# Stick-breaking attention's causal mask: moved from TensorE's products to a GpSimd multiplication

## The reference

```python
for blk in range(T // Q_BLOCK):            # Q_BLOCK = 128 queries
    s0 = blk * Q_BLOCK
    end = s0 + Q_BLOCK
    logits = jnp.einsum("bhtd,bhsd->bhts", q[:, :, s0:end], kb) * (Dh ** -0.5)
    mask = s_idx[None, :] < t_idx[:, None]
    log_keep = jnp.where(mask, jax.nn.log_sigmoid(-logits), 0.0)
    after = jnp.sum(log_keep, axis=-1, keepdims=True) - jnp.cumsum(log_keep, axis=-1)
    wts = jnp.where(mask, jnp.exp(jax.nn.log_sigmoid(logits) + after), 0.0)
    outs.append(jnp.einsum("bhts,bhsd->bhtd", wts, vb))
```

## Time and profile before

| | |
|---|---|
| Median of 3 runs | 1159.59 us (1159.42 to 1159.63) |
| The profiled execution | 1159.38 us, of which the trace's span is 1157.6 us |
| Busy share of the span | PE 96%, PEld 76%, DVE 45%, ACT 44%, POOL 32% |
| Mean granted TensorE clock | 0.991 of full speed |
| First and last of the 64 products with `bandbf` | start at 622.2 and 692.0 us |
| Loads of 1 MB into `raw` for `w_out_b` | 5.2 us from issue to landing |
| ScalarE's split of `D_OUTB + 1`, slot 1 | starts at 721.5 us |

### The profile page before, as it was taken

The page is one execution under the profiler, slowest core; times in us unless marked ns, Lnnn a source line. Parts: engine busy times, 40 slices in busy tenths (PEclk is TensorE's granted clock), DMA queues, the critical chain, the costliest instruction groups (busy, mean ns, idle before and its releaser), DMA issues.

```text
span 1157.6 us, 20420 instructions
## 1 busy us (share of the span) xinstructions
PE 1114.9 (96%) x8466; PEld 879.9 (76%) x8466; DVE 516.1 (45%) x938; ACT 514.7 (44%) x907; POOL 371.1 (32%) x148
## 2 busy tenths in 40 slices
PE   5999999989999999999999999999999999999998
PEld 3688886767768889777776668888877777678767
DVE  4575553455543366242234882853013332331562
ACT  5223226753335534453365883433335434753530
POOL 0134342232246341434334001333343213433260
PEclk7999999999999999999999999999999999999999
DMA  9822331276751132234522101322232322224201
GB/s 315 261 69 83 109 100 46 73 256 210 231 185 38 38 109 64 83 98 139 128 73 73 38 1 37 109 86 79 91 102 59 107 80 72 75 79 156 97 1 73
DMA packets 103004, 119.32 MB, mean 103 GB/s; under 512 B 4679, under 2 KB 89207, under 8 KB 102791
## 3 DMA queue, kind: packets, MB, share of 16 engines
q1 hardware_dynamic: 99054, 115.08, 31.4%
q10 hardware_dynamic: 3864, 3.01, 0.9%
HBM read 110.75 MB, written 2.10 MB: 97 GB/s over the span
## 4 chain that ended last, share of the span: by engine, by line
PE 83%; ACT 6%; DVE 5%; issue 3%; DMA 1%; ACTq 1%; SPq 0%; POOL 0%; DVEq 0%
PE ps L2079 43%; PE ps L2876 4%; PE ps L2125 2%; PE ps L2472 2%; PE ps L2686 2%; PE ps L2721 2%; PE ps L2498 2%; PE ps L2163 1%; PE ps L2704 1%; PE ps L2220 1%; PE ps L2243 1%; PE ps L2296 1%; PE ps L2842 1%; PE ps L2829 1%; DMA ada_a<-in_w_ada_dram 1%
## 5 line engine op out<-in xcount | busy, mean ns | idle before, releaser
L615 POOL TENSOR_TENSOR wlo<-raw,whi 128x2048 fp32r<-128x2048 f32 x53 | 245.3, 4629 | 525.6 <-ACT whi L781 513.1
L781 ACT ACTIVATE whi<-raw 128x2048 fp32r<-128x2048 f32 x52 | 99.3, 1912 | 191.7 <-PE ps L2079 152.6
L621 POOL TENSOR_TENSOR wlo<-raw,whi 128x2048 fp32r<-128x2048 f32 x10 | 46.4, 4639 | 112.0 <-ACT whi L870 63.5
L1809 DVE TENSOR_TENSOR_SCAN taken<-kept,taken 128x255 f32<-128x255 f32 (+2 forms) x64 | 51.2, 852 | 21.4 <-ACT taken L1200 21.4
L1290 ACT ACTIVATE p<-sc,nmx 128x256 f32<-128x256 f32 x64 | 32.0, 501 | 45.9 <-PE ps L2829 44.7
L1906 DVE CUSTOM_DVE_ANT_0 sc<-ps,biast 128x256 f32<-128x256 f32 (+1 forms) x64 | 22.4, 393 | 65.7 <-PE ps L2818 36.8
L870 ACT ACTIVATE whi<-raw 128x2048 fp32r<-128x2048 f32 x11 | 21.1, 1917 | 63.2 <-PE ps L2079 63.2
L2079 PE MATMUL ps<-hC_hi,whi 128*128 128x512 f32 x184 | 47.0, 397 | 0.8 <-POOL wlo L615 0.8
L2079 PE MATMUL ps<-hC_lo,whi 128*128 128x512 f32 x184 | 45.5, 390 | 0.0
L2079 PE MATMUL ps<-hC_hi,wlo 128*128 128x512 f32 x184 | 45.4, 389 | 0.0
L2079 PEld LDWEIGHTS ps<-hC_hi,whi 128*128 128x128 f32 x184 | 33.7, 188 | 14.8 <-issue 6.4
(11 more groups left out here) (504 smaller groups left out, 2641.9 us busy)
## 6 DMA issues: line engine op xcount, KB each, us to landing
raw<-in_w_in_dram SPq DMA_DIRECT2D x24, 1024.0 KB, 5.1
raw<-in_w_in_a_dram SPq DMA_DIRECT2D x16, 1024.0 KB, 5.6
raw<-in_w_ada_dram SPq DMA_DIRECT2D x8, 1024.0 KB, 5.1
late_w<-in_w_ada_dram SPq DMA_DIRECT2D x8, 1024.0 KB, 5.7
raw<-in_w_kv_dram SPq DMA_DIRECT2D x8, 1024.0 KB, 5.2
raw<-in_w_in_b_dram SPq DMA_DIRECT2D x8, 1024.0 KB, 6.0
ada_a<-in_w_ada_dram SPq DMA_DIRECT2D x4, 1024.0 KB, 10.2
ada_b<-in_w_ada_dram SPq DMA_DIRECT2D x4, 1024.0 KB, 12.9
```

What stands on the lines that cost most here:

```text
L615: pool.tensor_tensor(wlo[:, s, :], raw[:, s, :], whi[:, s, :].bitcast(F32), ALU.subtract).then_inc(lo_ready, 1)
L621: pool.tensor_tensor(wlo[:, s, :], raw[:, s, :], whi[:, s, :].bitcast(F32), ALU.subtract).then_inc(lo_ready, 1)
L781: A(whi[:, s, :], raw[:, s, :], ACT.Copy).then_inc(hi_ready, 1)
L1809: last = dve.tensor_tensor_scan(taken[:, r % 3, keys], kept[:, r % 3, keys], taken[:, r % 3, keys], 0.0, ALU.mult, ALU.add)
```

## The change

The mask no longer goes through the logits. TensorE's products with `bandbf` are left out, with the two casts that made that tile and the wait on them. Instead GpSimd multiplies the diagonal tiles of `taken` by a table of 0 and 1 (`earlier`, 1 where the key is before the query), in place, for both heads in one instruction, and VectorE's scans wait for `masked` where they waited for `taken_done`. `kept` isn't masked any more: over the masked keys the scan's state is still 0, whatever `kept` holds there. In GpSimd's queue the 24 rounds of masks stand between `split_lo(D_OUTB, 0)` and `split_lo(D_OUTB, 1)`.

```diff
-for _name, _n in (("ident", 128), ("band", 128), ("eps", 1), ...
+for _name, _n in (("ident", 128), ("earlier", 128), ("eps", 1), ...
...
-    put("band", np.where(p < c, 0.0, -BIG))
+    put("earlier", p > c)
...
-        bandbf = sb("bandbf", [128, 2, 128], BF16)
...
+            def mask(r):
+
+                pool.wait_ge(taken_done, r + 1)
+                for i, at in round_tiles(r):
+                    keys = of_round(taken, r)[:, :, at + 128 * i:at + 128 * i + 128]
+                    last = pool.tensor_tensor(keys, keys, C("earlier").unsqueeze(1).broadcast_to([128, 2, 128]), ALU.mult)
+                last.then_inc(masked, 1)
+
             split_lo(D_OUTB, 0)
+            for r in range(ROUNDS):
+                mask(r)
             split_lo(D_OUTB, 1)
...
             dve.wait_ge(cst_loaded, 16)
-            copy(bandbf[:, 0, :], ident)
-            copy(bandbf[:, 1, :], C("band")).then_inc(bf_ready, 1)
...
-            dve.wait_ge(bf_ready, 3)
+            dve.wait_ge(bf_ready, 2)
...
                 dve.wait_ge(kept_done, r + 1)
-                dve.wait_ge(taken_done, r + 1)
+                dve.wait_ge(masked, r + 1)
...
             pe.wait_ge(kqn_done, 16)
-            pe.wait_ge(bf_ready, 1)
...
                     for e in range(2):
-                        mm(logits(r)[:, e, at:at + 128 * i + 128], qTb[side(e), kt, 128 * i:128 * i + 128],
+                        last = mm(logits(r)[:, e, at:at + 128 * i + 128], qTb[side(e), kt, 128 * i:128 * i + 128],
                            kTb[side(e), kt, 0:128 * i + 128], start=at == 0, stop=True, skip_group_check=True)
-                for i, at in round_tiles(r):
-                    for e in range(2):
-                        last = mm(logits(r)[:, e, at + 128 * i:at + 128 * i + 128], bandbf[:, 1, :], bandbf[:, 0, :],
-                                  start=False, stop=True, skip_group_check=True)
                 last.then_inc(scores_full, 1)
```

More of the change, by code:

```diff
@@ L31 @@
 _at = 0
-for _name, _n in (("ident", 128), ("band", 128), ("eps", 1), ("first32", 1), ("ones", 128), ("onesbd", 128), ("tri", 128), ("half0", 128), ("half1", 128),
+for _name, _n in (("ident", 128), ("earlier", 128), ("eps", 1), ("first32", 1), ("ones", 128), ("onesbd", 128), ("tri", 128), ("half0", 128), ("half1", 128),
                   ("decmask", 64), ("m1t", 64), ("id64", 64), ("lev", 32 * len(LEVELS)), ("negtri", 128), ("negones", 128), ("swap", 128),
@@ L426, in mixer_stack @@
         picks_ready, last_silu = sem("picks_ready"), sem("last_silu")
-        cz_done = sem("cz_done")
+        cz_done, masked = sem("cz_done"), sem("masked")
         v_moved = [sem(f"v_moved{s}") for s in range(2)]
```

## The result

The changed kernel took 1170.59 us (median of 4 runs, 1168.9 to 1172.9), the kernel before 1159.51 us (4 runs, 1158.83 to 1159.63): a ratio of 1.0093, 95% interval 1.0078 to 1.0108. It is slower by some 11 us. The forecast was 1167.2 us, in a range of 1161.0 to 1170.5; the direction held, and the median lies 3.4 us above the forecast, at the upper end of the range (0.1 us beyond it).

The account below looks back on a forecast made before the run. TensorE bounds the kernel before, at 8.62 us a pair; VectorE and GpSimd together become the bound. Start and pairs +1.5, queueing at the end +4.35, clock +1.8 give +7.65, 1167.2 us against the median; range 1161 to 1170.5.

Parts of the forecast that it names:

- Exclusion of two-input instructions: Attention loop: GpSimd masks exclude VectorE's scans and `yb_low`, but not `yb`; an inserted mask costs 0.50 us.
- the list of signs: What would show it: scans in rounds 3 to 22 taking 0.5 us or more over their old 1.2, 0.94 and 0.6.
- the layout: One head pair retimed from A's first scan (rounds A: r % 3 = 0, then B, C), masks inserted: 9.26 us.
- Rival 1: Attention loop: masks hidden, TensorE still the bound, pairs of 7.9 us, about 1155 us in all; chance 0.06.
- TensorE would need 7.85 us a pair: Attention loop: dropping 64 bf16 products takes 0.77 us per pair off TensorE's 8.62.
- The pair: Attention loop: a head pair takes 9.2 us instead of 8.62, five pairs adding 2.9 us.
- The start, -1.4: Start of the loop: the split leaves, some masks come in; round 6's scans start at 644.2 instead of 645.58 us.
- The end, 4.35 us of queueing: End of the loop: `split_lo(D_OUTB, 1)` runs right behind round 23's masks, before its scans; 4.35 of +5.85 us.
- Rival 2: End of the loop: VectorE keeps the port through round 23's scans, the last split waits, clock stays; 1161.5 us, chance 0.08.
- The clock, 1.8 us: Behind the loop's end: TensorE idles 5.7 us, then half of 3.44 busy us at clock 0.50 is lost; +1.8 us.
- SP's load and the casts at 0: SP's load into `raw` slot 1 moving from 636 to 701 us, and dropping the two starting casts, each change nothing: 0.
- Rival 3: Attention loop: no overlap, every mask falls where VectorE waits, pairs of 10.0 us, about 1171.2 us; chance 0.08.

Follow-up runs that it names:

- the first experiment: Changed kernel with one wait more: GpSimd's `split_lo(D_OUTB, 1)` waits for the scans of round 23; 1164.15 us, ratio to before 1.0041.
- The merged instruction: Changed kernel with its last split behind the scans, and round C's two masks made in one GpSimd instruction over 128x512; 1161.72 us, a pair of 8.80 us.

## Why the prediction was right in direction and too low

1. **Exclusion of two-input instructions** held in all three forms: scans and `yb_low` stretched beside masks, masks stretched beside them, and `yb` (one input in PSUM) not. The last of these the changed kernel doesn't show, since no mask stands beside a `yb` there; the first experiment does (0.67 us at 700.89, beside the split from 701.05). An inserted mask of 0.73 us cost C's scans 0.48, where the forecast had 0.50: less than its length, and nothing on top of it. Only C's scans grew, by 0.48 us, and not those of all rounds by 0.5 or more as the list of signs had it; the layout itself had that right. The masks' handover of 0.07 to 0.1 us held too. Rival 1 (masks hidden) is out.
2. **TensorE would need 7.85 us a pair** failed. Without any mask a pair takes 8.38, with TensorE busy 8.11. The step subtracted the products' 0.77 us from the chain, and two thirds of it come back, in the pieces behind them and as short waits. It didn't reach the forecast's sum, since VectorE and GpSimd set the pair there; it would have made rival 1 too low.
3. **The pair: 9.2 taken, 9.26 laid out, 9.49 measured.** The layout was right in nearly every place. `taken` of B was to be ready at 2.1 us and was at 2.14; B's scans were to start at 3.0 and did at 3.04; `taken` of C at 4.3, measured 4.25. Only `taken` of the next A came later, at 664.53 + 1.02 - 657.65 = 7.90 for 7.5, which cost nothing, as its mask still fell among C's scans. The mis-sized term is C's two masks, 1.05 us between B's scans and C's besides `yb_low`: measured (664.25 - 662.40) - 0.59 = 1.26. A mask takes 0.72 and not 0.66, and the layout let both go in one stretch where `yb_low` got between them. The merged instruction bears the place out. Choosing 9.2 rather than 9.26 lost the rest. Five pairs: 4.35 us instead of 2.9.
4. **The start, -1.4**, came out +0.04: round 6's scans started at 648.16 - 2.54 = 645.62, before at 645.58. The gain from the split was real, 1.38 us where it alone was moved. What the forecast had too small was the masks there: `taken(2)` came at 635.00 - 2.54 = 632.5 and not 632.1, since dropped products save little; its masks took 1.41 us and ended at 636.47 - 2.54 = 633.9, 0.5 late. And rounds 3 to 5, for which the forecast had 8.25 us (635.95 to 644.2), took about 9.2: they carried masks of 0.87, 1.28 and 1.99 us (GpSimd's timeline of the loop's start). That the forecast worked out no layout for these three rounds is its weakest place. With the pairs this is the largest error, 1.4 us.
5. **The end, 4.35 us of queueing**, was right, place and mechanism: 4.69 measured by the same sum (9.07 - 4.38), and 4.2 by undoing it; the other 0.5 are the masks of the last pair. Rival 2 is out.
6. **The clock, 1.8 us**, measured 1.91, with 3.64 us of busy TensorE at 0.50 where the earlier trace rows had 3.44.
7. **SP's load and the casts at 0** held: ScalarE's split of that slot starts at 735.04 us, before at 721.52, apart by the 13.52 us of all that lies before them, and both times it waits for TensorE and not for the load. No gain from the casts shows: at 330 us the changed kernel is 0.34 us later than before, the first experiment 0.62 earlier.
8. **Rival 3** (no overlap, pairs of 10.0 us) had 1171.2 us, nearer to the measured 1170.59 than the forecast's 1167.2. That is luck: its pairs are 0.5 us longer than the measured ones, and its start of -1.4 us wasn't there either. Those two errors, +2.6 us in the pairs and -1.4 at the start, mostly cancel.

The sum made again with what was measured is 4.38 + 4.69 + 1.91 = 10.98, where the forecast had 1.5 + 4.35 + 1.8 = 7.65. Of the 3.3 us between them, 1.4 are the start, 1.45 the pairs, 0.34 the end and 0.1 the clock.

What stays open is why the pieces of TensorE behind a dropped product lengthen; no run took that apart. That masks and scans hold each other up where both read SBUF is shown by the versions without reads and without the wait; that a ring through ScalarE's queue then sets the 9.49 us is read from the chain of waits, and the later versions fit it.

## What to carry to other kernels

Work moved to an idle engine isn't free when that engine and the one that waits for it shut each other out: look for the long instruction beside which a short one stood still, and lay the loop out with it. Then read every place in the queue behind the inserted work. Here a 4.5 us split that had been harmless came to stand behind the last mask, cost 4.2 us and 1.9 us of clock, and one wait put it right. Insert work where the consumer is off the ring (round A), and where a waiting instruction could get in between, in one instruction rather than two; don't count what is dropped from the bounding engine at its full length.

## What the runs showed of the hardware that I had not expected

- A GpSimd instruction directly behind another starts before VectorE, released by the first, gets in: split at 702.05, scans at 702.20, which ended only 1.76 us after the split.
- Two GpSimd instructions of 128x256 leave room for a waiting VectorE one between them (2.18 us for the two, `yb_low` 1.15); one of 128x512 doesn't (1.62 and 1.69).
- Memsets on GpSimd leave two-input instructions of VectorE alone; a multiplication that reads SBUF makes `yb_low` 0.48 us longer.
- Dropping 0.77 us of bf16 products between f32 ones took 0.44 us off TensorE's busy time.
